# Building the Strassen weight sums by chains of 32 transfers, and interleaving two quads at the opening of the MLP

## The reference, cut to what matters

```
h = rmsnorm(x);  z = h @ w_in                        # 46 weight tiles of 128 columns, after 16 for keys and values
A = retention(q, k, v from z, rotary on q and k);  B = rwkv7(...)
x = x + merge(A, B) @ w_out
x = x + cross_attention(rmsnorm(x)) @ w_co
hm = rmsnorm(x)
x = x + square(relu(hm @ w_up)) @ w_down             # hidden width 4096
y = rmsnorm(x)
```

## Time and profile before

| | before |
|---|---|
| median of 3 runs | 2273.63 us (2272.64 to 2275.64) |
| profiled execution, its own time | 2272.92 us |
| its span in the trace | 2270.9 us |
| PE busy | 2189.9 us (96%) |
| DVE, ACT, POOL busy | 47%, 23%, 20% |
| mean granted TensorE clock | 0.993 |

### The profile page before, as it was taken

One profiled execution on the slowest core, in us unless ns is written; L12 is line 12 of the kernel. 1 busy time (PEld: TensorE's weight loads), 2 busy tenths in 40 slices (PEclk: granted clock), 3 DMA queues, 4 the chain that ended last, 5 costly groups with the idle time before them and its releaser, 6 DMA issues.

```text
span 2270.9 us, 49259 instructions
## 1 busy us (share of the span) xinstructions
PE 2189.9 (96%) x21418; PEld 2068.3 (91%) x21418; DVE 1070.9 (47%) x1530; ACT 530.4 (23%) x1010; POOL 457.1 (20%) x380
## 2 busy tenths in 40 slices
PE   8999999999999988999999999998999999999997
PEld 6899888888888888979999987988999999999997
DVE  5333744636445345262544145366445354454455
ACT  4111434224342211154011023122102011021023
POOL 0233201112021033223333200231111111111110
PEclk9999999999999999999999999999999999999999
DMA  7433514335053299537113125112122122122122
GB/s 303 147 124 137 138 37 92 78 69 131 19 113 75 45 268 253 142 104 300 46 46 115 43 86 193 47 47 65 57 63 77 54 68 71 52 75 64 58 75 79
DMA packets 92999, 230.20 MB, mean 101 GB/s; under 512 B 10912, under 2 KB 26656, under 8 KB 90016
## 3 DMA queue, kind: packets, MB, share of 16 engines
q1 hardware_dynamic: 62944, 156.22, 20.8%
q0 software_dynamic: 19136, 46.14, 10.0%
q10 hardware_dynamic: 10752, 25.35, 3.1%
HBM read 199.62 MB, written 74.19 MB: 121 GB/s over the span
## 4 chain that ended last, share of the span: by engine, by line
PE 84%; DVE 6%; DMA 3%; ACT 2%; issue 2%; SPq 2%; POOL 0%; ACTq 0%; DVEq 0%; POOLq 0%
PE ps L514 84%; DMA w_raw<-w 2%; DVE F L1431 2%; SPq L2759 2%; ACT F L2224 1%; DMA vc<-vc 1%; DVE Xst L1431 0%; DVE F L1437 0%; DVE F L1434 0%; DVE Sst L1434 0%; ACT L2224 0%; DVE xtf L1437 0%; DMA z<-zstg 0%; DMA par<-par 0%; POOL w_split L451 0%
## 5 line engine op out<-in xcount | busy, mean ns | idle before, releaser
L514 PE MATMUL ps<-A_s,w_split 128*128 128x364 f32 (+1 forms) x3888 | 699.4, 336 | 16.3 <-POOL w_split L451 12.7
L514 PEld LDWEIGHTS ps<-A_s,w_split 128*128 128x128 f32 x3888 | 648.1, 189 | 43.3 <-POOL w_split L451 13.6
L514 PE MATMUL ps<-hid,msp 128*128 128x364 f32 (+3 forms) x2304 | 385.5, 329 | 0.0
L514 PEld LDWEIGHTS ps<-hid,msp 128*128 128x128 f32 x2304 | 382.4, 188 | 1.7 <-issue 0.5
L449 POOL CAST w_split<-w_raw 128x1024 fp32r<-128x1024 f32 x78 | 85.5, 1096 | 1104.1 <-PE ps L514 805.8
L514 PE MATMUL ps<-B_s,w_split 128*128 128x364 f32 (+1 forms) x1728 | 288.2, 328 | 0.5 <-POOL w_split L451 0.5
L514 PEld LDWEIGHTS ps<-B_s,w_split 128*128 128x128 f32 x1728 | 286.7, 188 | 0.8 <-issue 0.8
L1431 DVE TENSOR_TENSOR F<-ps,F 128x1092 f32<-128x1092 f32 (+3 forms) x84 | 104.3, 1241 | 347.7 <-PE ps L514 347.7
L506 POOL CAST msp<-mraw 128x512 fp32r<-128x512 f32 x176 | 117.7, 670 | 619.5 <-PE ps L514 606.9
L514 PE MATMUL ps<-xb,msp 128*128 128x272 f32 x1536 | 203.7, 291 | 8.9 <-DVE hidf L1437 4.5
L514 PEld LDWEIGHTS ps<-xb,msp 128*128 128x128 f32 x1536 | 199.0, 191 | 9.6 <-DVE hidf L1437 4.7
(11 more groups left out here) (247 smaller groups left out, 2427.6 us busy)
## 6 DMA issues: line engine op xcount, KB each, us to landing
sums_up<-w POOLq DMA_DIRECT2D x44, 1024.0 KB, 9.4
w_raw<-w SPq DMA_DIRECT2D x80, 512.0 KB, 3.7
mraw<-w SPq DMA_DIRECT2D x112, 256.0 KB, 2.6
mraw<-sums_up SPq DMA_DIRECT2D x64, 256.0 KB, 2.6
z<-zstg SPq DMA_DIRECT2D x83, 182.0 KB, 2.1
F<-z SPq DMA_DIRECT2D x16, 546.0 KB, 9.1
w_raw<-w SPq DMA_DIRECT2D x7, 1024.0 KB, 10.4
kc<-kc SPq DMA_DIRECT2D x7, 1024.0 KB, 4.9
```

What stands on the lines that cost most here:

```text
L514: return pe.matmul(out, lhsT, rhs, start=start, stop=stop, skip_group_check=skip)
```

## The change

1. **Sums (POOL).** 32 transfers in place of 44. Each group now takes 8: copies S1 <- A21 and S3 <- A11 (n = 0 to 7); accumulating S1 += A22 and S3 += A21 (n = 8 to 15); then by n = 16 to 31 a copy S2 <- S1, S2 += A11, a copy S4 <- S2, S4 += A12, each behind a wait for the one before it in its group. No sum is started behind tiles 32 to 45. SP's final wait counts 8 for each group.
2. **Order of products (PE, SP, POOL).** `OPENING` has the last six as 6, 6, 7, 7, 4, 4 of quads 0 and 1 in turn, in place of 6, 7, 4 of quad 0 and then of quad 1. The accumulators of each product stay as they were. `OPENED` is changed alike, so that the fourth block of quad 0 is number 6, and `down` waits for seven `lo`.
3. **Token sums.** T2 was F\*g + xb.hi in four DVE instructions and + xb.lo in a fifth; now ACT writes F\*g into T3's place in four instructions, and DVE adds xb.hi and xb.lo in two wide ones. T3 is made from the same place in four DVE instructions (F\*g - T3), and its former fifth instruction falls away. T4 stays.
4. **c12.** The block was acc3 - (acc6 - P1); now it is (acc3 + P1) - acc6, with the first part (`c12_early`) ahead of product 6. DVE's and ACT's lists are put into the new order.

```
-        OPENING = ((0, 1), (0, 5), (0, 2), (0, 3), (1, 1), (1, 5), (1, 2), (1, 3), (0, 6), (0, 7), (0, 4), (1, 6), (1, 7), (1, 4))
+        OPENING = ((0, 1), (0, 5), (0, 2), (0, 3), (1, 1), (1, 5), (1, 2), (1, 3), (0, 6), (1, 6), (0, 7), (1, 7), (0, 4), (1, 4))
...
-        OPENED = ((0, 0, 0), (1, 0, 0), (0, 0, 1), (0, 1, 1), (0, 1, 0), (1, 0, 1), (1, 1, 1), (1, 1, 0))
+        OPENED = ((0, 0, 0), (1, 0, 0), (0, 0, 1), (1, 0, 1), (0, 1, 1), (1, 1, 1), (0, 1, 0), (1, 1, 0))
...
             def sum_step(n):
-                if n < 16:
-                    to_sum(n // 4, n % 4, 1, 0, False)
+                if n < 8:
+                    put(n // 2, (S1, S3)[n % 2], up_block(n // 2, *(A21, A11)[n % 2]))
+                elif n < 16:
+                    g, j = (n - 8) // 2, n % 2
+                    if j == 0:
+                        pool.wait_ge(d_sum[g], 16 * 2)
+                    plus(g, (S1, S3)[j], up_block(g, *(A22, A21)[j]))
                 elif n < 32:
-                    g, j = (n - 16) // 4, n % 4
-                    if j == 0:
-                        pool.wait_ge(d_sum[g], 16 * issued[g])
-                    to_sum(g, (0, 1, 3, 2)[j], int(j < 3), int(j < 3), True)
-                elif n < 40:
-                    g, j = (n - 32) // 2, n % 2
-                    if j == 0:
-                        pool.wait_ge(d_sum[g], 16 * issued[g])
-                    to_sum(g, (1, 3)[j], 0, 0, True)
-                elif n < 44:
-                    g = n - 40
-                    pool.wait_ge(d_sum[g], 16 * issued[g])
-                    to_sum(g, 3, 0, 1, True)
+                    g, stage = n % 4, (n - 16) // 4
+                    pool.wait_ge(d_sum[g], 16 * (4 + stage))
+                    if stage == 0:
+                        put(g, S2, sum_block(g, S1))
+                    if stage == 1:
+                        plus(g, S2, up_block(g, *A11))
+                    if stage == 2:
+                        put(g, S4, sum_block(g, S2))
+                    if stage == 3:
+                        plus(g, S4, up_block(g, *A12))
...
-                        pe.wait_ge(m_lo, BEFORE + 5)
-                        pe.wait_ge(m_b, BEFORE + 3 + 3 * t)
+                        pe.wait_ge(m_lo, BEFORE + 7)
+                        pe.wait_ge(m_b, BEFORE + 5 + t)
...
+                def c12_early(self):
+                    self.done(3)
+                    tt(halves(self.block(0, 1)), self.acc[3], halves(self.block(1, 0)), ALU.add).then_inc(m_c, 1)
+
+                def c12_late(self):
+                    self.done(6)
+                    self.count(m_c, 1, 1)
+                    tt(halves(self.block(0, 1)), halves(self.block(0, 1)), self.acc[6], ALU.subtract).then_inc(m_b, 1)
+                    self.count(m_b, 3, 1)
+                    squeezed(self.block(0, 1), halves(self.block(0, 1)), 1)
...
+                lows(2)
+                v.wait_ge(t_hi, BEFORE_R + 1)
+                own.add(tt(T2, T3, f32(xb[:, 1, :, 0, :]), ALU.add))
+                lows(3)
                 own.wait()
                 tt(T2, T2, f32(xb[:, 1, :, 1, :]), ALU.add).then_inc(t_sum, 1)
-                unit_lo(0, 0, 4)
+                v.wait_ge(rs_ready, 4)
+                q0.c11()
+                lows(4, 5)
                 q0.both_sums()
...
+                q0.c12_early()
+                lows(8)
                 own.wait()
+                v.wait_ge(t_sum, BEFORE + 3)
                 tok_lo(0)
...
+                q1.c11()
+                lows(9, 10)
+                tok_lo(1)
+                q0.c12_late()
+                q1.both_sums()
+                lows(11)
+                q1.c12_early()
                 own.wait()
+                q1.c12_late()
                 tok_lo(2)
+                lows(12)
+                q0.c22()
                 lo(0)
...
+                lows(13)
                 lo(1)
...
+                q1.c22()
+                lo(2)
                 q0.c21()
...
+                lows(14)
                 lo(3)
...
                 lo(4)
...
+                q1.c21()
+                lows(15)
                 lo(5)
...
                 lo(6)
+                lows(16)
                 lo(7)
+                lows(17)
...
+                for k in range(4):
+                    ins = act(xtf[:, 1, k, 1, :], F[:, 4 + k, HT:T], ACT.Copy, scale=col("gmlp", 4 + k))
+                ins.then_inc(t_hi, 1)
                 kept(0, 0, True, 0, 5)
```

More of the change, by code:

```diff
@@ new lines, in _, with put, plus @@
+            S1, S2, S3, S4 = range(4)
+            def put(g, kind, src):
+                pool.dma_start(sum_block(g, kind), src).then_inc(d_sum[g], 16)
+            def plus(g, kind, src):
+                pool.dma_start(sum_block(g, kind), src, accum_op=ALU.add).then_inc(d_sum[g], 16)
+            def sum_step(n):
+                if n < 8:
[5 more added lines that the diff above has]
+                    plus(g, (S1, S3)[j], up_block(g, *(A22, A21)[j]))
+                elif n < 32:
+                    g, stage = n % 4, (n - 16) // 4
[8 more added lines that the diff above has]
+                        plus(g, S4, up_block(g, *A12))
@@ L2030, in __init__ @@
                 def __init__(self, i, o, first, q):
-                    self.i, self.o, self.first, self.q, self.n = i, o, first, q, 4 * o + q
+                    self.i, self.o, self.first, self.q, self.n = i, o, first and q < 2, q, 4 * o + q
                     self.acc = [ACC_OF, FIRST_ACC[q % 2]][first and q < 2]
@@ L2040, in count @@
                 def count(self, s, per, k):
-                    v.wait_ge(s, self.i * 4 * per + (BEFORE + per * self.n + k))
+                    if self.first and s is m_b:
+                        v.wait_ge(m_b, BEFORE + 2 * k - 1 + self.q)
+                    else:
+                        v.wait_ge(s, self.i * 4 * per + (BEFORE + per * self.n + k))
                 def both_sums(self):
@@ L2083, in tok_lo, with lows @@
                 def tok_lo(x):
-                    v.wait_ge(t_hi, BEFORE_R + x + 1)
+                    v.wait_ge(t_hi, BEFORE_R + x + 2)
                     tt(xt[:, x, :, 1, :], xtf[:, x, :, 1, :], f32(xt[:, x, :, 0, :]), ALU.subtract).then_inc(t_lo, 1)
[L2087 to L2090, removed]
+                def lows(*ls):
+                    for l in ls:
+                        unit_lo(0, 0, l)
@@ L2091, in opening @@
+                lows(2)
+                v.wait_ge(t_hi, BEFORE_R + 1)
+                own.add(tt(T2, T3, f32(xb[:, 1, :, 0, :]), ALU.add))
+                lows(3)
                 own.wait()
                 tt(T2, T2, f32(xb[:, 1, :, 1, :]), ALU.add).then_inc(t_sum, 1)
-                unit_lo(0, 0, 4)
+                v.wait_ge(rs_ready, 4)
+                q0.c11()
+                lows(4, 5)
                 q0.both_sums()
-                unit_lo(0, 0, 5)
+                for k in range(4):
+                    ins = stt(T3[:, k, :], F[:, k, HT:T], col("gmlp", k), T3[:, k, :], ALU.mult, ALU.subtract)
+                    if k < 3:
+                        own.add(ins)
+                    else:
+                        ins.then_inc(t_sum, 1)
@@ L2096, in opening @@
+                lows(6, 7)
                 v.wait_ge(t_sum, BEFORE + 1)
                 for k in range(4):
[L2098 to L2101, removed]
+                    ins = stt(T4[:, k, :], F[:, 4 + k, 0:HT], col("gmlp", 4 + k), T2[:, k, :], ALU.mult, ALU.subtract)
+                    if k < 3:
+                        own.add(ins)
+                    else:
+                        ins.then_inc(t_sum, 1)
@@ L2102, in opening @@
+                q0.c12_early()
+                lows(8)
                 own.wait()
+                v.wait_ge(t_sum, BEFORE + 3)
                 tok_lo(0)
[L2104 to L2107, removed]
-                own.wait()
-                tt(T3, T3, f32(xb[:, 3, :, 1, :]), ALU.subtract).then_inc(t_sum, 1)
@@ L2674, in tok_hi @@
             def tok_hi(x):
+                a.wait_ge(t_sum, BEFORE + x + 1)
                 act(xt[:, x, :, 0, :], xtf[:, x, :, 1, :], ACT.Copy).then_inc(t_hi, 1)
@@ L2704, in opening @@
                 kept(0, 0, True, 1, 1)
-                a.wait_ge(t_sum, BEFORE + 2)
                 tok_hi(1)
+                kept(0, 0, True, 1, 5)
                 tok_hi(2)
-                kept(0, 0, True, 1, 5)
-                for z in range(1, 8):
+                squared(0, 1, *OPENED[1])
+                for z in range(2, 8):
                     squared(0, z, *OPENED[z])
```

42 lines of the change are left out of this document (8 added, 34 removed).

## The result

The changed kernel takes 2252.40 us (median of 4 runs, 2249.96 to 2254.50) against 2274.13 us of the kernel before (4 runs, with one more than above): ratio 0.9904, interval 0.9887 to 0.9921, so 21.7 us or 1.0% faster. Forecast were 23.8 us and 2250. The profiled execution took 2253.22 us with a span of 2251.4, 19.5 us under that of before. These 19.5 us are read off the trace first.

A forecast was written before the change was run, and what follows sets the result against it. PE bounds the kernel, busy 2189.9 of 2270.9 us, so only its idle time and low-clock loss can be regained. 15.5 + 8.3 + 1 - 1 = 23.8 us gave 2249.8, say 2250 us; 8 in 10 range 2243 to 2264.

The forecast's parts named there:

- Full DMA stretch: PE's waits for split weight tiles at 833 to 873 us: 15.5 us gained with their clock loss, bounds 9 and 17.
- leftovers: Waits for split tiles and retention's inputs that may remain after the sums go: 1.3 us subtracted from 16.8.
- one of its signs: Between 830 and 875 us, PE's three waits for `w_split` gone or down to 2 us, the clock there at 1.00.
- the cautious 856: Landing time of the third weight tile's load if distances from 806 shrink to 0.8, by bytes; it came at 868.4 before.
- cast and remainder: POOL's split of a loaded weight tile: takes 3.5 us, so each load is needed that much before PE wants the tile.
- What is late next: At retention's start, rotation of q and k and `Vr` come late from the same queue: some 0 to 4 us given back.
- `lw`: At 247.73 us its load shares the engines with the accumulation of n = 15: 0 to 3.6 us lost, 1 taken.
- Idle time at 708: PE's 3.13 us idle at 708.48, behind the removed accumulation of n = 32: 0 to 2 us back, 1 taken.
- the small terms: Ahead of the full DMA stretch: 1 us back at 708 us against 1 us lost at the load of `lw`.
- The opening: MLP start, first product to `down`: `down` 10.1 us earlier, less 1.8 us of clock, net 8.3 us, bounds 4 and 11.
- the third rival: MLP opening: late POOL casts add up to 18 us to DVE's chain, a loss of 10 us, 2268 us; chance 0.05.
- the two large terms: 15.5 us from the waits for split tiles at 833 to 873 us and 8.3 us net from the MLP's opening.

## Why the prediction was right, point by point

- **Full DMA stretch, forecast 15.5 us, measured 9.1 in the profiled pair.** The mechanism stands: the tiles were late by the engine time of POOL's sums, shown by giving back traffic of two kinds. The term was too large. What was allowed for leftovers was 1.3 us; the third tile cost 3.68 us and 1.6 of clock (18 matmuls in 4.58 in place of 3.0 us), and the new waits for the stores of `zstg` 2.2 us, which the prediction had not named though the stores stood on the same engines: 16.8 - 5.3 - 2.2 = 9.3. So one of its signs, waits down to 2 us and a clock of 1.00, was not met at the third tile. The third load landed at 855.6, near the cautious 856. The pair understates it: the stretch takes 66.2 to 71.9 us over the ten traces with 32 transfers, 69.3 on average, and 80.1 and 82.7 us in the two kernels with the 44 sums, so the mean gain is some 12 us. The changed kernel itself took 71.0 and 66.2: one trace of the stretch is not exact to better than some 5 us.
- **How long a split takes.** The prediction gave cast and remainder 3.5 us. Of the 3.68 us at the third tile 1.7 us are because they took 855.61 to 860.81, 5.2 us. In the changed trace they take 1.04 and 2.38 to 2.40 us when DVE rests (806.75, 838.80), and 1.86 to 2.07 and 3.26 to 3.33 us while DVE rotates q and k (821.00, 855.61), whose operations take up to 3.48 in place of 1.29 us there. The trace of before has the same two kinds (2.34 and 3.27 us for the remainder). That they hold each other up is read from these coincidences; no run took one of them away.
- **What is late next.** Named was the rotation of q and k. It is what PE waits for at retention's start, 1.2 to 3.4 us, in six of the ten traces with 32 transfers, a second trace of the changed kernel among them; in the first PE had no such wait.
- **`lw`, forecast a loss of 1 of 0 to 3.6 us, measured 2.9** (0.49 to 3.39), from the accumulation of n = 15: shown by its removal.
- **Idle time at 708, forecast 1 us back, measured 3.1, and 4.0 with the clock behind it.** It was 3.13 and 3.41 us in the two kernels with the accumulation of n = 32, 2.63 with that given back, 1.39 with a copy there, and at most 0.85 in those without a transfer. That it hangs on the traffic is shown; that it is fetching of instructions is only argued. A second one at 566 us, 2.00 and 1.60 us in the two kernels with the 44 sums and in no other, was not named at all. So the small terms, forecast at 0 in sum, gave 3.3 us in the pair, 2.0 on average over the traces that have the wait for `lw`.
- **The opening, forecast 8.3 us net, measured 5.9.** Right in kind: no PE stall over 1.03 us ahead of the last product, one of 5.37 us (forecast 5.2) before `down`, DVE busy for 47.52 of 47.86 us. `down` started 8.5 us earlier after the first product, not 10.1, since DVE's list took 47.9 instead of 46.4 us. The 46.4 took over the lengths of the old list. In the new one nine instructions are longer than their like by 0.3 to 0.4 us each (three remainders of units 1.09 to 1.10 in place of 0.68, a wide one 2.83 in place of 2.41), against five in the old. The clock behind the wait cost 11.76 - 9.19 = 2.6 us up to the first F sum, not 1.8; but over the nine traces with this idle time it cost 1.5 to 2.6, median 1.7, so here the forecast had the usual size, and the opening gained up to 7 us in others.
- **Cast and DVE excluding each other.** POOL's casts in the new opening took 0.61 to 1.68 us, shorter at the top than the 3.62 of before, though DVE has no pause. So the third rival fell: DVE waited for no cast, and PE for no unit. But the rule of the Trainium skill, "SBUF — State Buffer", "Who interferes with whom", is borne out in kind, and not only for POOL: each of DVE's nine long instructions runs beside a cast of POOL, and together they make its list, on which `down` waits, 3.5 us longer than at the short forms (1.9 in the old list), which is where the forecast's 1.5 us went. That too is read from the trace, and no run shows it apart.
- **Sum.** Forecast were 15.5 + 8.3 + 0 = 23.8 us. In the profiled pair it is 9.1 + 5.9 + 3.3 + 0.9 (behind retention's start) = 19.2 of the span's 19.5 us; the medians differ by 21.7 us with an uncertainty of some 4. The mechanisms were right, and the forecast lies within the uncertainty of the times, but that it came so near was in part luck: the two large terms were too high in the same direction, both having been taken as if nothing else became late, and small terms that nobody had forecast made up part of it. By the means over all traces it is some 12 us in the full stretch, 2 ahead of it, 1 behind it and 6.7 in the opening (70.7 to 64.0 us), which comes to the 21.7 us of the medians.

## What to carry to other kernels

When an engine waits for a load, ask what else is on the DMA engines at that time, and count in engine time, not in bytes: here an accumulating transfer cost the engines about twice as much as a copy of as many bytes. Background transfers belong where the engines have room, and not just ahead of a small load that something waits for. Where two engines alternate over accumulators, the order of the slower one's list is the schedule: look at the last item that the faster one needs, and put whatever isn't needed by then behind it. And before you subtract two places of two traces, make sure that the same instruction stands at both.

## What the runs showed of the hardware that was not expected

- After 5.37 us of idle time before `down` the granted clock was 0.50 for the next 4.8 us, so 1.2 GHz, and the F sum came 2.6 us later than at full clock. Over nine traces with this idle time the clock of these 4.8 us was 0.50 to 0.68 and the loss 1.5 to 2.6 us. After 2.74 us in the same place it was 1.00 in one trace, but 0.71 after 2.73 us in another, and 0.64 after 2.26 us in a third, with losses of 1.3 and 1.6 us. So idle time here cost its own length and, but for one trace, a quarter to seven tenths of it more, and a shorter one did not reliably save the clock.
- Twelve accumulations of 1 MB, of which 3.80 MB fell into the 67 us of the full stretch, put POOL's queue at 31.8% of the engines' time there; twelve copies of the same size, with 4.19 MB in it, at 16.5%. They took 1903 and 1088 packets.
- An idle time of PE that the profile files under issue was three different things here: at 708 us it went with traffic on the DMA engines, before `down` it was a wait for a semaphore of DVE, and at retention's start it ended with DVE's last rotation.
- POOL's split of a weight tile took 3.4 us beside a resting DVE (1.04 and 2.38 us), and 4.7 to 5.4 us where DVE rotated q and k the while (1.44 and 3.27 at 868.44 in the trace of before, 2.07 and 3.33 at 821.00 in the changed one).
